# Moving the half swaps and the GELU steps of the S5 stream behind the attention steps in two engine queues

## Chip, cores and metric

The kernel runs on one core of a Trainium2 chip. The metric is the device time of one execution in microseconds (us); the figure of a kernel is the median of its runs.

## What is computed

A trunk of two residual layers over 2048 tokens of width 1024, with an RMSNorm at the end. The change touches only layer 0 (the even layer). It projects the normed input with one weight matrix and feeds two groups of heads:

```python
proj = h @ ev_w_in[i]
u, g_a, q, k, v, g_b = split_cols(proj, [...])
a_out = s5_mixer(u, ...) * jax.nn.silu(g_a)
b_out = swa_mixer(q, k, v, sinks, rel_bias) * jax.nn.silu(g_b)
mix = jnp.concatenate([a_out, b_out], axis=-1) @ ev_w_out[i]
```

`s5_mixer` is a diagonal complex state-space recurrence in 32 groups of 16 channels, followed by a GELU and a gated linear unit. `swa_mixer` is attention in 32 chunks of 64 queries, each over 128 keys, with a sink in the softmax. Layer 1 is a gated linear attention layer.

## The kernel before, in words

Each engine has its own in-order program, written out by hand, and the engines meet through semaphores. In the even layer every engine runs the same loop over a step counter `p` (0 to 147). Two steps make one accumulation `n = p // 2` of the input projection: in each step TensorE (PE) issues 12 products of 128x512 (line 1089), in three passes of high and low halves. There are 72 accumulations, so steps 0 to 143 have products. The last eight groups of weights (accumulations 40 to 71) are gates: ScalarE (ACT) takes a tanh (L638) and VectorE (DVE) finishes the gate (`silu`, L936). Other accumulations are copied out by ACT (L634). Three PSUM banks hold accumulations.

Into this loop two other pieces of work are woven, placed by small functions of `p`.

**The S5 stream**, one group `i` every three steps (`stream_at`), with `S_IN(0) = 40` and `S_OUT(0) = 43`:

- step 40+3i: PE `inputs(i)` (L1125), ACT `take_v(i)` (L675, L676, swaps the halves), DVE `scan(i)` (L942 to L945);
- step 41+3i: ACT `take_z(i)` (L682, L683, swaps the halves of the scan's result), DVE `turn_back(i)` (L954 to L956, writes `pz`);
- step 43+3i: PE `outputs(i)` (L1132, L1133), which waits for `pz` of group i and for `gelu_out(i-1)`, since both use one PSUM bank; ACT `gelu_square(i)` (L687);
- step 44+3i: DVE `gelu_arg(i)` (L960), ACT `gelu_tanh(i)` (L691);
- step 45+3i: DVE `gelu_out(i)` (L966). SyncE stores the result a step later.

`outputs(i-1)` and `inputs(i)` thus stand in the same step, one behind the other. The output steps are 43, 46, ..., 136. SyncE issues `load_stream(i)` (L375 to L379) at step 37+3i, once `outputs(i-2)` is done.

**The attention**, one chunk `c` every two steps (`chunk_at`), with `2*A0 = 80`:

- even step 80+2c: PE `scores(c)` (L1148), DVE `maxima(c)` (L984 to L990), ACT `exponents(c)` (L696, L698);
- odd step 81+2c: DVE `sums(c)` (L996, L997), ACT `copy_v(c)` (L718) and `normalize(c)` (L705), PE `turn_v(c)` (L1158);
- odd step 83+2c: PE `turn_p(c)` (L1165), ACT `copy_turned(c)` (L712);
- even step 84+2c: PE `values(c)` (L1175), DVE `take(c)` (L1004).

From step 80 to step 138 both are under way, and the pattern of the two repeats every six steps. Steps 16 to 49 also hold the making of the S5 tables (`powers_of_b`, `powers_of_c`, `copy_bm`, `copy_ker`). On PE each step runs its products first, then `outputs`, `inputs`, `values`, `scores`, `turn_p`, `turn_v`, as far as the step has them.

Of the kernel before, what the change touches and what calls it, by code (L numbers as in the profile page):

```python
# [151 lines left out]
def even_layer(nc, prm, scr, ht_hi, ht_lo, cst):  # L152
# [10 lines left out]
    S_IN, S_OUT = (lambda s: 40 + 3 * s), (lambda s: 43 + 3 * s)  # L163
# [4 lines left out]
    stream_at = lambda p, base: (p - base) // 3 if (p - base) % 3 == 0 and 0 <= (p - base) // 3 < NGRP else None  # L168
# [25 lines left out]
    with ExitStack() as ctx:  # L194
# [116 lines left out]
        with nc.Block() as block:  # L311
# [269 lines left out]
            def _(act):  # L581
# [34 lines left out]
                def evacuate(n):  # L616
                    g, b = accs[n]
                    act.wait_ge(acc_full, n + 1)
                    if g < G_K:
                        h = half_of(g, b)  # L620
                        if n < 8 and b >= 2:
                            act.wait_ge(u_stored[h], 16)
                        elif n >= 8:
                            act.wait_ge(u_stored[h], 32 if g == 2 else 48)
                        if n == 1:
                            act.wait_ge(zero_in, 16)
                        out = ustage[:, h].rearrange("p (s c) -> p c s", s=TS)[:, b % 2 * GLU_C:(b % 2 + 1) * GLU_C, :]
                        a.copy(out, acc[n % 3][:].rearrange("p (c s) -> p c s", s=TS)).then_inc(acc_free, 1)
                    elif n < N_GATE0:
                        if n < 20:  # L630
                            act.wait_ge(u_stored[n % 4 // 2], 64)
                        else:
                            act.wait_ge(stored[n % 4], 16 * (n // 4 - 4))
                        a.copy(stage[:, n % 4], acc[n % 3][:]).then_inc(acc_free, 1)  # L634
                    else:
                        if n > N_GATE0:
                            act.wait_ge(acc_free, n)
                        a.activation(th[:], acc[n % 3][:], ACT.Tanh, scale=0.5).then_inc(th_done, 1)  # L638
# [39 lines left out]
                def take_z(i):  # L678
                    act.wait_ge(z_ready, i + 1)
                    if i:  # L680
                        act.wait_ge(pz_ready, i)
                    a.mul(z_sw[0:ST], z[ST:P], -1.0).then_inc(z_swapped, 1)  # L682
                    a.copy(z_sw[ST:P], z[0:ST]).then_inc(z_swapped, 1)  # L683

                def gelu_square(i):
                    act.wait_ge(y_done, i + 1)
                    a.activation(e[:], ps_y, ACT.Square, scale=math.sqrt(0.044715)).then_inc(squared, 1)  # L687
# [20 lines left out]
                def copy_turned(n):  # L708
                    act.wait_ge(p_turned, n + 1)
                    if n:  # L710
                        act.wait_ge(o_done, n)
                    a.copy(pt[:], ps_p).then_inc(pt_ready, 1)  # L712
# [31 lines left out]
                evacuate(5)  # L744
                for p in range(13, p_end):
                    n = p // 2
                    i = stream_at(p, S_IN(0) + 1)
                    if i is not None:
                        take_z(i)
                    if p % 2 == 1 and n < n_acc:  # L750
                        evacuate(n)
                    c_ = chunk_at(p, 2 * A0 + 3)
                    if c_ is not None:
                        copy_turned(c_)
                    c_ = chunk_at(p, 2 * A0 + 1)
                    if c_ is not None:
                        copy_v(c_)
                        normalize(c_)
                    q = batch_at(p, TB + 1)
                    if q is not None:  # L760
                        copy_bm(q)
                    q = batch_at(p, TB + 2)
                    if q is not None:
                        copy_ker(q)
                    if p == 14:
                        split(2)
                    if p % 2 == 0 and n % 4 == 2 and n >= 10 and n // 4 + 1 < N_GRP:
                        split(n // 4 + 1)
                    i = stream_at(p, S_OUT(0) + 1)
                    if i is not None:  # L770
                        gelu_tanh(i)
                    i = stream_at(p, S_OUT(0))
                    if i is not None:
                        gelu_square(i)
                    i = stream_at(p, S_IN(0))
                    if i is not None:
                        take_v(i)
                    c_ = chunk_at(p, 2 * A0)
                    if c_ is not None:
                        exponents(c_)  # L780

            @block.vector
            def _(dve):
# [174 lines left out]
                def gelu_arg(i):  # L958
                    dve.wait_ge(squared, i + 1)
                    d.scalar_tensor_tensor(e[:], e[:], 1.0, ps_y, ALU.add, ALU.mult).then_inc(arg_ready, 1)  # L960

                def gelu_out(i):
                    dve.wait_ge(tanh_done, i + 1)
                    if i >= 2:
                        dve.wait_ge(g_st[i % 2], 16 * (i // 2))
                    d.scalar_tensor_tensor(go[:, i % 2], e[:], 1.0, ps_y, ALU.add, ALU.mult).then_inc(g_ready, 1)  # L966
# [10 lines left out]
                def maxima(n):  # L977
                    b = n % 2
                    dve.wait_ge(s_done, n + 1)
                    if n == 0:  # L980
                        dve.wait_ge(bias_in, 128)
                    if n >= 2:
                        dve.wait_ge(p_turned, n - 1)
                    ach.link(d.scalar_tensor_tensor(s[:, b], ps_s, DH ** -0.5, bias[:], ALU.mult, ALU.add))  # L984
                    if n == 0:
                        ach.link(d.memset(s[:, b, :, 0:CHUNK], -1e30))
                    ach.link(d.tensor_reduce(mx[:, b], s[:, b], AX_X, ALU.max))
                    ach.link(d.tensor_tensor(mx[:, b], mx[:, b], sink, ALU.max))
                    ach.mark(d.tensor_tensor(sd[:, b], sink, mx[:, b], ALU.subtract))
                    ach.link(d.tensor_scalar(mmx[:, b], mx[:, b], -1.0, None, ALU.mult))  # L990
                    dve.sem_inc(m_ready, 1)
# [30 lines left out]
                    pass  # L1022
                for p in range(12, p_end):
                    n = p // 2
                    i = stream_at(p, S_OUT(0) + 2)
                    if i is not None:
                        gelu_out(i)
                    i = stream_at(p, S_OUT(0) + 1)
                    if i is not None:
                        gelu_arg(i)  # L1030
                    if p % 2 == 0 and 0 <= silu_of(n - 1) and n - 1 < n_acc:
                        silu(n - 1)
                    c_ = chunk_at(p, 2 * A0 + 1)
                    if c_ is not None:
                        sums(c_)
                    c_ = chunk_at(p, 2 * A0 + 4)
                    if c_ is not None:
                        take(c_)
                    c_ = chunk_at(p, 2 * A0)
                    if c_ is not None:  # L1040
                        maxima(c_)
                    if p == 15:
                        split(2)
                    if p % 2 == 1 and n % 4 == 2 and n >= 10 and n // 4 + 1 < N_GRP:
                        split(n // 4 + 1)
                    q = batch_at(p, TB)
                    if q is not None:
                        powers_of_b(q)
                    q = batch_at(p, TB + 1)
                    if q is not None:  # L1050
                        powers_of_c(q)
                    q = batch_at(p, TB + 3)
                    if q is not None:
                        skip(q)
                    if p == S_IN(0) - 3:
                        for k in range(2):
                            dve.wait_ge(cs_st[k], CS_ALL // 2)
                        ch.link(d.memset(pz[:], 0.0))
                    i = stream_at(p, S_IN(0) + 1)
                    if i is not None:  # L1060
                        turn_back(i)
                    i = stream_at(p, S_IN(0))
                    if i is not None:
                        scan(i)
                    if p == TB + 2 * NQ + 6:
                        clear_keys()
                    if p == TB + 2 * NQ + 8:
                        distances()
# [1251 lines left out]
```

## Time and profile before

| | before |
|---|---|
| median of 3 runs | 1899.45 us (1895.48 to 1900.75) |
| the profiled execution, its own time | 1895.48 us |
| its span, first to last instruction | 1893.7 us |
| granted TensorE clock, mean | 0.965 of full |
| PE matmul busy | 1704.9 us, 90% |
| DVE busy | 842.9 us, 45% |
| ACT busy | 617.9 us, 33% |
| even layer's products (L1089) | 50.6 to 636 us |

Busy shares are averages over stages with different limits. The profile page slices the span, its timeline lists instructions in order with the idle time before each and what ended it in square brackets, and its table of waits sums those by pair. Engine names: PE is TensorE's matmuls, PEld its weight loads, SPq the SyncE queue that issues DMAs.

### The profile page before, as it was taken

Reading aid. Unit: us, or ns where it says so; the run is one execution under the profiler, and the core shown is the slowest. Engines: PE = TensorE matmul, PEld = TensorE weight load, DVE = VectorE, ACT = ScalarE, POOL = GpSimd, SP = SyncE. Lnnn points to the kernel's source line nnn. Section 1 sums busy time; section 2 is a strip of 40 time slices with the busy share of each in tenths; the row PEclk is TensorE's granted clock in tenths of the full one; section 3 lists DMA queues with packets and bytes.
Section 4 is the critical chain, followed back from the end, with each engine's and each line's share of the span. In section 5 each row is a group of like instructions: output and inputs, shape, how many; then the busy total and the mean of one; then the engine's idle time right before and its main releaser. Section 6 shows DMA issues by size and latency. Waiting matters only on the chain. (4 is left out here: it accounts for less than half of the span.)

```text
span 1893.7 us, 23556 instructions
## 1 busy us (share of the span) xinstructions
PE 1704.9 (90%) x7814; PEld 1365.8 (72%) x7814; DVE 842.9 (45%) x1677; ACT 617.9 (33%) x1587; POOL 398.3 (21%) x519
## 2 busy tenths in 40 slices
PE   1998897899999582998969999999999999979998
PEld 1776676777777371776856788888888888868886
DVE  3868443366666355233323323343333444343443
ACT  3622232366666431232324312222222233131211
POOL 0776000000000031875810002221222121000000
PEclk9999998999999796998979999999999999989999
DMA  7435444444544497555522333333333332265653
GB/s 173 143 110 158 119 126 125 134 133 133 151 140 129 129 314 245 180 154 165 178 67 84 106 109 109 109 114 104 116 111 118 97 112 84 84 209 161 191 179 110
DMA packets 316482, 261.03 MB, mean 138 GB/s; under 512 B 84344, under 2 KB 260280, under 8 KB 316376
## 3 DMA queue, kind: packets, MB, share of 16 engines
q1 hardware_dynamic: 299896, 249.13, 42.7%
q10 hardware_dynamic: 16480, 10.56, 1.9%
q8 instruction: 58, 0.95, 0.2%
q14 instruction: 48, 0.39, 0.1%
HBM read 157.33 MB, written 102.30 MB: 137 GB/s over the span
## 5 line engine op out<-in xcount | busy, mean ns | idle before, releaser
L2149 PE MATMUL odd_acc<-ht_hi,odd_w_hi 128*128 128x512 f32 x800 | 333.8, 417 | 8.5 <-DVE odd_w_hi L1986 8.5
L2149 PE MATMUL odd_acc<-ht_lo,odd_w_hi 128*128 128x512 f32 x800 | 315.3, 394 | 0.0
L2149 PE MATMUL odd_acc<-ht_hi,odd_w_lo 128*128 128x512 f32 x768 | 299.8, 390 | 0.0
L1089 PE MATMUL ev_acc<-ht_hi,ev_w_hi 128*128 128x512 f32 x576 | 244.5, 424 | 1.4 <-DVE ht_lo L801 1.4
L1089 PE MATMUL ev_acc<-ht_lo,ev_w_hi 128*128 128x512 f32 x576 | 228.4, 397 | 0.0
L1089 PE MATMUL ev_acc<-ht_hi,ev_w_lo 128*128 128x512 f32 x576 | 228.0, 396 | 0.0
L2149 PEld LDWEIGHTS odd_acc<-ht_hi,odd_w_hi 128*128 128x128 f32 x800 | 151.2, 189 | 49.6 <-DVE odd_w_hi L1986 8.7
L2149 PEld LDWEIGHTS odd_acc<-ht_lo,odd_w_hi 128*128 128x128 f32 x800 | 150.8, 188 | 33.8
L2001 DVE TENSOR_TENSOR odd_stage<-odd_acc,rms_rows 128x512 f32<-128x512 f32 x96 | 66.4, 692 | 229.3 <-PE odd_acc L2149 229.3
L2149 PEld LDWEIGHTS odd_acc<-ht_hi,odd_w_lo 128*128 128x128 f32 x768 | 144.6, 188 | 28.6
L1591 PE MATMUL out_acc<-wo_hi,mix_hi 128*128 128x512 f32 x256 | 107.0, 418 | 46.5 <-POOL mix_lo L1483 40.4
L1089 PEld LDWEIGHTS ev_acc<-ht_hi,ev_w_hi 128*128 128x128 f32 x576 | 110.5, 192 | 26.1 <-issue 3.3
L1303 POOL TENSOR_TENSOR glu_g_lo<-glu_g,glu_g_hi 128x2048 fp32r<-128x2048 f32 x4 | 22.2, 5539 | 508.7 <-ACT glu_g_hi L1315 508.7
L1089 PEld LDWEIGHTS ev_acc<-ht_lo,ev_w_hi 128*128 128x128 f32 x576 | 110.2, 191 | 24.9
L1089 PEld LDWEIGHTS ev_acc<-ht_hi,ev_w_lo 128*128 128x128 f32 x576 | 110.6, 192 | 21.3
L1915 ACT ACTIVATE odd_gl_o<-odd_gl_ps_o_s 128x256 f32<-128x256 f32 x64 | 24.6, 384 | 242.4 <-DVE odd_gl_state L2057 229.0
L1591 PE MATMUL out_acc<-wo_hi,mix_lo 128*128 128x512 f32 x256 | 102.7, 401 | 0.0
L1591 PE MATMUL out_acc<-wo_lo,mix_hi 128*128 128x512 f32 x256 | 102.7, 401 | 0.0
L1591 PEld LDWEIGHTS out_acc<-wo_hi,mix_hi 128*128 128x128 f32 x256 | 50.0, 195 | 60.1 <-POOL mix_lo L1483 41.7
L1857 POOL TENSOR_TENSOR odd_gl_var<-odd_gl_sumsq,odd_eps 128x1 f32<-128x1 f32 x64 | 21.8, 341 | 338.5 <-ACT odd_gl_o L1915 338.5
L1480 POOL TENSOR_TENSOR mix_hi<-mix_raw,xo_ones 128x1024 fp32r<-128x1024 f32 x32 | 76.5, 2391 | 62.7 <-PE out_acc L1591 46.4
L1507 ACT ACTIVATE ht_hi<-out_turned,xo_norm 128x128 f32 x128 | 36.5, 368 | 135.2 <-PE out_turned L1603 135.2
(297 smaller groups left out, 3172.9 us busy)
## 6 DMA issues: line engine op xcount, KB each, us to landing
odd_gl_in<-scr_heads SPq DMA_DIRECT2D x32, 640.0 KB, 4.3
mix_raw<-scr_mix SPq DMA_DIRECT2D x32, 512.0 KB, 4.1
scr_heads<-odd_stage SPq DMA_DIRECT2D x64, 256.0 KB, 2.0
odd_w_raw<-od_w_in SPq DMA_DIRECT2D x48, 256.0 KB, 3.5
ev_w_raw<-ev_w_in SPq DMA_DIRECT2D x36, 256.0 KB, 4.5
ev_x_tile<-x SPq DMA_DIRECT2D x16, 512.0 KB, 3.8
ev_s_cos_sin<-scr_s_cos_sin SPq DMA_DIRECT2D x32, 256.0 KB
xo_tile<-x SPq DMA_DIRECT2D x32, 256.0 KB, 4.5
```

Source lines behind the costliest of these rows:

```text
L1089: mm = pe.matmul(acc[n % 3][:], w[j][:, k, :], h[:, k, t], start=(k == 0 and r == 0), stop=(k == KT - 1 and r == 2))
L1303: nc.gpsimd.tensor_tensor(in_steps(g_lo[n % 2][:]), g[:, n], in_steps(g_hi[n % 2].ap().bitcast(F32)), ALU.subtract).then_inc(split, 1)
L1480: nc.gpsimd.tensor_tensor(m_hi[j][:], raw[:, j], ones[:].unsqueeze(1).broadcast_to([P, KT, P]), ALU.mult).then_inc(m_hi_done, 1)
L1507: m = nc.scalar.activation(ht_hi[:, KH * h + k, ds(t * P, P)], pt[j][:, k * P:(k + 1) * P], ACT.Copy, scale=norm_col[:, KH * h + k:KH * h ...
L1591: m = pe.matmul(acc[j][:], mt[j][:, k], wt[:, k], start=(k == 0 and q == 0), stop=(k == KT - 1 and q == 2))
L1857: g.tensor_tensor(var[:, j:j + 1], ss[:, j:j + 1], eps[:], ALU.add).then_inc(var_done, 1)
L1915: s.activation(on[:, j], ps_o[j], ACT.Square, scale=DV ** -0.5, accum_out=ss[:, j:j + 1]).then_inc(ss_done, 1)
L2001: v.tensor_tensor(stage[:, n % 4], acc[n % 4][:], rb[:, t], ALU.mult).then_inc(acc_free, 1)
L2149: mm = pe.matmul(acc[n % 4][:], w[j][:, k, :], h[:, k, t], start=(k == 0 and q == 0), stop=(k == KT - 1 and q == len(passes) - 1))
```

## The change

On ACT, `take_z` moves from the front of the step to a place behind the evacuation, the attention copies, the normalization, the table copies, the weight split, `gelu_tanh` and `gelu_square`; only `take_v` and `exponents` stand behind it. On DVE, `gelu_out` and `gelu_arg` move from the front of the step to a place behind `silu`, `sums`, `take` and `maxima`; `turn_back` and `scan` stay where they are, at the end. No instruction is added or removed, no wait is changed, and each of them stays in its step.

```diff
@@ ACT, for p in range(13, p_end)
-                    i = stream_at(p, S_IN(0) + 1)
-                    if i is not None:
-                        take_z(i)
                     if p % 2 == 1 and n < n_acc:
                         evacuate(n)
...
                     i = stream_at(p, S_OUT(0))
                     if i is not None:
                         gelu_square(i)
+                    i = stream_at(p, S_IN(0) + 1)
+                    if i is not None:
+                        take_z(i)
                     i = stream_at(p, S_IN(0))
                     if i is not None:
                         take_v(i)
@@ DVE, for p in range(12, p_end)
-                    i = stream_at(p, S_OUT(0) + 2)
-                    if i is not None:
-                        gelu_out(i)
-                    i = stream_at(p, S_OUT(0) + 1)
-                    if i is not None:
-                        gelu_arg(i)
                     if p % 2 == 0 and 0 <= silu_of(n - 1) and n - 1 < n_acc:
                         silu(n - 1)
...
                         maxima(c_)
+                    i = stream_at(p, S_OUT(0) + 2)
+                    if i is not None:
+                        gelu_out(i)
+                    i = stream_at(p, S_OUT(0) + 1)
+                    if i is not None:
+                        gelu_arg(i)
```

## Rows read from the trace of the kernel before

**Rows 1.** Busy time by stretch, with instructions in brackets, clock and DMA share.
```profile
core 0: us, PE busy (x) PEld busy (x) DVE busy (x) ACT busy (x) POOL busy (x), PEclk, DMA share, GB/s
400.00:500.00 100.00, 99.23 (x473) 76.00 (x472) 65.69 (x173) 66.72 (x233) 0.00 (x0) 1.00 0.48 143
```

**Rows 2.** PE's waits from 190 to 640 us: total us, times, longest.
```profile
PE ev_bank L1125 <- DMA ev_s_u<-scr_u: 17.7, 5, 9.6
PE ev_bank L1116 <- DVE ev_s_cpow L916: 4.7, 2, 4.0
```

**Rows 3.** Timeline of PE, 450 to 480 us: start, duration; products left out.
```profile
451.57 0.67 PE L1132 MATMUL ev_bank<-ev_s_u,ev_s_tables 128*128 128x256 f32 x2
...
453.62 1.13 PE L1148 MATMUL ev_bank<-ev_at_keys,ev_at_q 128*128 128x256 f32 x4
...
461.01 0.65 PE L1175 MATMUL ev_bank<-ev_at_probs_turned,ev_at_v_by_key 128*64 128x256 f32 x4 [0.18 <-issue]
...
465.32 0.59 PE L1132 MATMUL ev_bank<-ev_s_u,ev_s_tables 128*128 128x256 f32 x2
...
466.61 0.60 PE L1165 MATMUL ev_bank<-const_ident,ev_at_scores 128*128 128x128 f32 x4
...
477.66 0.67 PE L1132 MATMUL ev_bank<-ev_s_u,ev_s_tables 128*128 128x256 f32 x2
```

**Rows 4.** Timeline of ACT, 450 to 480 us.
```profile
467.77 0.57 ACT L712 COPY ev_at_probs_turned<-ev_bank 128x512 f32<-128x512 f32 x1
...
470.36 0.38 ACT L676 ACTIVATE ev_s_v_swapped<-ev_bank 64x256 f32<-64x256 f32 x1
472.75 0.42 ACT L682 ACTIVATE ev_s_z_swapped<-ev_s_z 64x256 f32<-64x256 f32 x1 [2.01 <-DVE ev_s_z L945]
...
473.62 0.42 ACT L691 ACTIVATE ev_s_gelu<-ev_s_gelu 128x256 f32<-128x256 f32 x1
475.84 0.20 ACT L696 ACTIVATE ev_at_small<-ev_at_small 128x4 f32<-128x4 f32 x1 [1.80 <-DVEq L991]
...
477.49 0.57 ACT L638 ACTIVATE ev_gate_tanh<-ev_acc 128x512 f32<-128x512 f32 x1
...
479.77 0.37 ACT L687 ACTIVATE ev_s_gelu<-ev_bank 128x256 f32<-128x256 f32 x1
```

**Rows 5.** Timeline of DVE, 450 to 480 us.
```profile
454.79 0.69 DVE L984 SCALAR_TENSOR_TENSOR ev_at_scores<-ev_bank,ev_at_bias 128x512 f32<-128x512 f32 x1 [0.63 <-PE ev_bank L1148]
...
456.82 0.42 DVE L942 TENSOR_TENSOR ev_s_v_turned<-ev_bank,ev_s_cos_sin 128x256 f32<-128x256 f32 x1
...
458.68 0.39 DVE L960 SCALAR_TENSOR_TENSOR ev_s_gelu<-ev_s_gelu,ev_bank 128x256 f32<-128x256 f32 x1
...
472.94 0.68 DVE L936 SCALAR_TENSOR_TENSOR ev_stage<-ev_gate_tanh,ev_acc 128x512 f32<-128x512 f32 x1
...
473.87 0.68 DVE L984 SCALAR_TENSOR_TENSOR ev_at_scores<-ev_bank,ev_at_bias 128x512 f32<-128x512 f32 x1
...
475.96 0.43 DVE L954 TENSOR_TENSOR ev_s_pz<-ev_s_z,ev_s_cos_sin 128x256 f32<-128x256 f32 x1 [0.21 <-DVE ev_at_small L990]
...
477.10 0.41 DVE L966 SCALAR_TENSOR_TENSOR ev_s_out<-ev_s_gelu,ev_bank 128x256 f32<-128x256 f32 x1
477.62 0.16 DVE L996 TENSOR_TENSOR ev_at_small<-ev_at_small 128x4 f32<-128x4 f32 x1
...
478.10 0.69 DVE L936 SCALAR_TENSOR_TENSOR ev_stage<-ev_gate_tanh,ev_acc 128x512 f32<-128x512 f32 x1
```

**Rows 6.** The SyncE queue's waits, 190 to 640 us.
```profile
SPq L375 <- PE ev_bank L1133: 33.5, 16, 4.3
```

**Rows 7.** Timeline of PE: two stalls, in brackets.
```profile
239.50 0.61 PE L1116 MATMUL ev_bank<-ev_s_cpow,ev_s_bbar 128*16 128x128 f32 x4 [3.98 <-DVE ev_s_cpow L916]
...
317.39 0.70 PE L1125 MATMUL ev_bank<-ev_s_u,ev_s_tables 128*128 128x256 f32 x2 [1.47 <-DMA ev_s_u<-scr_u]
```

**Rows 8.** Busy time by stretch, right behind those two stalls; PEclk is the granted clock.
```profile
239.50:242.00 2.50, 2.50 (x9) 1.89 (x10) 1.91 (x8) 0.84 (x3) 0.00 (x0) 0.68 0.62 194
...
317.30:320.00 2.70, 2.61 (x11) 2.18 (x12) 1.04 (x3) 0.74 (x2) 0.00 (x0) 1.00 0.63 215
```

## The prediction

> **What bounds the kernel now.** I read the busy time by stretch first. While S5 stream and attention run together PE is busy 99.2% of the time at full clock, against 66% for DVE and ACT [rows 1]. The even layer is bound by PE there, and a reordering of ACT and DVE can win only PE's idle time, or make some. PE's table of waits comes next: from 190 to 640 us it waits 17.7 us in 5 stalls for stream inputs from DMA and 4.7 us in 2 for the S5 tables [rows 2]. These lie ahead of the attention or at its edge. Inside it the timeline shows 0.18 us ahead of one `values` in each cycle of six steps [rows 3]. So at most some 2 us are to be won in the cycles, and the question is how much room PE's next operands have. The timelines of the three engines over one cycle answer it.
>
> The tightest operand is that of `outputs`, which needs `pz` and the preceding `gelu_out`. In the cycle shown `outputs` starts at 477.66 [rows 3]; its `gelu_out` starts at 477.10 and lasts 0.41 [rows 5], so it ends 0.15 us before. What the change puts ahead of `gelu_out` beyond 0.15 us becomes a stall of PE, once PE can't go around it.
>
> **The change part by part.** Nothing is added, so each engine's busy time stays. Ends move. Two kinds of `outputs` alternate, since three steps change the parity.
>
> *Intervals before.* From `outputs` in an odd step to the next, in an even step: 477.66 - 465.32 = 12.34 us, without a wait in it. From an even one to the next odd one: 465.32 - 451.57 = 13.75 us, with the 0.18 us in it [rows 3]. A cycle is 26.09 us.
>
> *Interval odd to even, after.* Count from the start of `outputs` (0). `turn_p` starts at 466.61 - 465.32 = 1.29 and ends at 1.89 [rows 3]. `copy_turned` starts at 1.93, and from there `copy_v`, `normalize`, `gelu_square` and `take_v` run on ACT in 470.74 - 467.77 = 2.97 us [rows 4]: 4.90. `scan` takes 458.68 - 456.82 = 1.86 from 4.93: 6.79. In the next (even) step DVE now begins with `silu` and `take`, 473.87 - 472.94 = 0.93: 7.72; from the start of `maxima` to whatever follows it are 475.96 - 473.87 = 2.09: 9.81 [rows 5]. PE's scores are ready before that (they end some 6.4 us after `outputs`), so they don't set it. Up to here little is new. What follows is: `gelu_arg` starts only now, 0.39 and 0.03 of handing on: 10.23. ACT has waited for it, although the maxima were ready, because `gelu_tanh` stands ahead of `exponents` in its queue. `gelu_tanh` 0.41: 10.64; `take_z` 473.62 - 472.75 = 0.87: 11.51 [rows 4]; then `exponents`, and `sums` 477.62 - 475.84 = 1.78 after their start [rows 4, 5]: 13.29; `sums` 0.48: 13.77; `gelu_out`, now behind `sums`, 0.41 and 0.04: 14.22. Before, `exponents` went straight behind `maxima`, and `gelu_out` did not wait for them at all. PE would be ready at 12.34: a stall of **1.88 us**.
>
> *Interval even to odd, after.* `scores` starts 453.62 - 451.57 = 2.05 after `outputs` and `maxima` 1.17 after that: 3.22 [rows 3, 5]. `exponents` follow `maxima`'s start by 475.84 - 473.87 = 1.97: 5.19, and hold ACT for 1.65: 6.84. In the odd step `evacuate`, `copy_turned`, `copy_v`, `normalize` take 479.77 - 477.49 = 2.28: 9.12 [rows 4]. `scan` and `sums` on DVE end before `normalize` starts (3.22 + 3.89 + 0.48 = 7.59), `gelu_arg` right behind. Then `gelu_tanh` 0.41 and `take_z` 0.87: 10.40. `take_z` used to go ahead of the four. What it delays is `turn_back`: 10.43 plus 477.10 - 475.96 = 1.14: 11.57 [rows 5]. `silu` and `take` 0.93: 12.50; `maxima` 2.09: 14.59; `gelu_out`, which used to go ahead of these three, 0.45: 15.04. Against 13.75 this is **1.29 us** more, the 0.18 us for `values` won back in it already, since `copy_turned` and `copy_v` no longer stand behind `take_z`.
>
> *How many.* Even output steps under attention: 82, 88, ..., 136, ten. Odd ones: 85, ..., 133, nine. The first one (82) has no `silu` or `take` ahead of it and I take 0.5 us less. Sum: 10 x 1.88 - 0.5 + 9 x 1.29 = 29.9 us. A stall also lets the others catch up, but that is in the count already: it runs around from `outputs` to `outputs`, and the cycle is then 29.3 us and no longer PE's. I left out the weight splits, 1 us on ACT and DVE every eighth step; in the new order they fall into time in which the engine waits. What is queued behind the late `gelu_out` and `take_z`: on DVE `split`, `turn_back`, `scan`; on ACT `take_v`, `exponents`. All are in the count. SyncE's store of the S5 result and the next `load_stream` move with `outputs`, and keep their three steps.
>
> *Steps 40 to 79.* Without attention `gelu_out` and `gelu_arg` have nothing new ahead of them. `take_z` goes behind an evacuation (0.48) and `gelu_tanh` (0.41) in an odd step, but has two more steps of PE's products before `outputs`, over 5 us: nothing. With the tables (41, 44, 47) it goes behind `copy_bm` or `copy_ker` too, while PE's table waits total 4.7 us [rows 2]. Bounds: 1 us won (evacuations and copies earlier), 3 lost (1 us each, if a `turn_back` pushes out a table step). I take 0, nearest to what the stalls show: they end with DVE steps that stay ahead of `turn_back`.
>
> *Clock.* After a stall of 1.47 us the granted clock is 1.00, that is 2.4 GHz; after one of 3.98 us it is 0.68 over 2.5 us, part of it at 1.2 GHz [rows 7, 8]. The stalls expected are at the first kind, so the sum has nothing for it. The Trainium skill ("TensorE: Matmul & The Clock Gate", section "A second HAM failure mode: psum-queue depth-cycling") tells of a kernel whose TensorE idled only briefly but often between groups of matmuls and whose clock still swung between its two levels. By the row the clock costs nothing here, by that rule it costs the second rival's price below.
>
> **Rivals.** (1) *Only one side stalls.* The even-to-odd chain has 22 steps and exceeds PE by 1.3 us; with 0.05 us less at each hand-over it is 1 us shorter and nearly hidden, and 18 to 20 us remain: 1914. For it: my ACT durations are ends, and the next instruction starts some 0.1 us earlier; against: the chain reproduces what the trace shows before `maxima`. (2) *The clock falls.* After the 3.98 us stall 9 matmuls were issued in 2.5 us where full clock has some 12.5 [rows 8], so twice 3.5 matmuls in 5 us, at 0.23 us 1.6 us a stall: with 19 stalls 30 us more, 1956. Against it: the stall of 1.47 us. (3) *The other side: faster.* `evacuate` no longer waits behind `take_z`, SyncE's stores and with them its queue move up, stream loads arrive earlier, and part of the 17.7 us goes away [rows 2]; all of it would give 1878. It decides if those loads are issued late because of a store ahead of them. Against it: SyncE's wait at the head of the load is for `outputs` on PE, 33.5 us in 16 [rows 6]. And it would have to outweigh the stalls. (4) *Nothing happens:* other limits I misread leave `gelu_out` in time, as in steps 40 to 79; then only 2 us are won, 1894 in the profiled execution. Against it: the 0.15 us.
>
> **How the numbers follow.** The profiled execution took 1895.48 us; with 30 it gives 1925.4. The median of the three runs is 4.0 us above it, which gives 1929.4. I say 1928. The forecast (both sides stall, clock full) has 0.78, rival 1 0.08, rival 2 0.07, rival 3 0.03, rival 4 0.04. Chain lengths uncertain by 0.6 us each make 19 x 0.6 = 11 us, the table steps -1 to +3, runs 4: 1912 to 1946, which takes in rival 1 and leaves out the others. Differences within 0.3% (5.7 us) can't be told from none. Slower by more: 0.92; within: 0.05; faster: 0.03.
>
> **What would show it.** In the changed kernel's PE waits, L1132 should wait for DVE's `gelu_out` 19 times, about 1.9 and 1.5 us in turn, some 30 us in all; the 0.18 us ahead of `values` should be gone; even outputs should follow each other by 29.3 us; the exponents should start 1.7 us later after the maxima in every third attention step; `gelu_out` should start right behind `sums` or `maxima`. Steps before 80 should take as long as before, with the same DMA stalls, and everything after the even layer should only shift. PEclk should stay at 10 tenths between 370 and 660 us. The prediction is wrong if `outputs` waits for `pz` rather than `gelu_out`, if the clock falls behind these stalls, or if the stalls by DMA grow or vanish.

## The result

The changed kernel takes 1929.12 us (median of 4 runs, 1926.30 to 1931.81) against 1900.10 us for the one before (4 runs): a ratio of 1.0157 (95% interval 1.0136 to 1.0180), 30 us slower. The profiled execution took 1925.92 us with a span of 1924.1 us, 30.4 us more than before. The forecast of 1928 us and its direction held.

The profile after, first by stretch. The busy times of PE, DVE and ACT in the attention stage are what they were; only the stage is longer:

```profile
370.00:670.00 300.00, 267.79 (x1264) 202.81 (x1262) 173.02 (x460) 177.95 (x630) 0.00 (x0) 1.00 0.40 117
```

The granted clock, third from the end, is 1.00 over all of it. The same stretch of the kernel before, up to 640 us, holds 266.23 us of PE work. Where the 30.4 us arise is told by the start of `outputs` in its last step ahead of the attention (step 79: 353.91 us after, 355.11 before) and in its very last step (136: 638.56 after, 608.25 before). Between the two lie 284.65 us after and 253.14 before: the stage is 31.5 us longer, 1.2 us were gained ahead of it, and 0.1 us arises behind it.

PE's waits from 190 to 690 us, as [rows 2] (total, times, longest):

```profile
PE ev_bank L1132 <- DVE ev_s_out L966: 30.5, 19, 1.7
PE ev_bank L1125 <- DMA ev_s_u<-scr_u: 17.9, 5, 8.9
PE ev_bank L1116 <- DVE ev_s_cpow L916: 4.5, 2, 3.6
```

The first row is new: `outputs` (L1132) waits for `gelu_out` (L966), 19 times, 30.5 us. The other two are as in [rows 2]. Three `outputs` in a row in the timeline of PE, as in [rows 3]:

```profile
462.30 0.67 PE L1132 MATMUL ev_bank<-ev_s_u,ev_s_tables 128*128 128x256 f32 x2 [1.69 <-DVE ev_s_out L966]
...
477.46 0.67 PE L1132 MATMUL ev_bank<-ev_s_u,ev_s_tables 128*128 128x256 f32 x2 [1.53 <-DVE ev_s_out L966]
...
491.67 0.67 PE L1132 MATMUL ev_bank<-ev_s_u,ev_s_tables 128*128 128x256 f32 x2 [1.70 <-DVE ev_s_out L966]
```

Even to odd 15.16 us (13.75 before), odd to even 14.21 us (12.34 before), a cycle of 29.37 us (26.09 before). The way from an odd to an even `outputs`, on ACT and then on DVE, as in [rows 4, 5]:

```profile
482.08 0.38 ACT L676 ACTIVATE ev_s_v_swapped<-ev_bank 64x256 f32<-64x256 f32 x1
487.73 0.42 ACT L691 ACTIVATE ev_s_gelu<-ev_s_gelu 128x256 f32<-128x256 f32 x1 [5.28 <-DVE ev_s_gelu L960]
488.18 0.42 ACT L682 ACTIVATE ev_s_z_swapped<-ev_s_z 64x256 f32<-64x256 f32 x1
488.62 0.40 ACT L683 COPY ev_s_z_swapped<-ev_s_z 64x256 f32<-64x256 f32 x1
489.05 0.20 ACT L696 ACTIVATE ev_at_small<-ev_at_small 128x4 f32<-128x4 f32 x1
```

```profile
485.26 0.68 DVE L984 SCALAR_TENSOR_TENSOR ev_at_scores<-ev_bank,ev_at_bias 128x512 f32<-128x512 f32 x1
...
487.28 0.42 DVE L960 SCALAR_TENSOR_TENSOR ev_s_gelu<-ev_s_gelu,ev_bank 128x256 f32<-128x256 f32 x1
...
490.83 0.16 DVE L996 TENSOR_TENSOR ev_at_small<-ev_at_small 128x4 f32<-128x4 f32 x1 [0.55 <-ACT ev_at_scores L698]
491.03 0.18 DVE L997 RECIPROCAL ev_at_small<-ev_at_small 128x4 f32<-128x4 f32 x1
491.12 0.40 DVE L966 SCALAR_TENSOR_TENSOR ev_s_out<-ev_s_gelu,ev_bank 128x256 f32<-128x256 f32 x1
```

ACT is idle for 5.28 us, with `take_z` and then the exponents queued behind; it waits for `gelu_arg` (L960), which DVE runs behind the maxima (L984). Only then come `gelu_tanh` (L691), `take_z` (L682, L683) and the exponents (L696), 3.79 us after the maxima's start instead of 1.97 [rows 4, 5]. `sums` (L996) wait for the exponents, `gelu_out` stands behind them, ends at 491.52, and PE starts at 491.67.

The way from an even to an odd `outputs`, from 462.30 to 477.46:

```profile
467.49 0.21 ACT L696 ACTIVATE ev_at_small<-ev_at_small 128x4 f32<-128x4 f32 x1 [1.77 <-DVEq L991]
...
471.43 0.41 ACT L691 ACTIVATE ev_s_gelu<-ev_s_gelu 128x256 f32<-128x256 f32 x1
```

```profile
472.74 0.43 DVE L954 TENSOR_TENSOR ev_s_pz<-ev_s_z,ev_s_cos_sin 128x256 f32<-128x256 f32 x1 [1.54 <-ACT ev_s_z_swapped L683]
...
476.89 0.42 DVE L966 SCALAR_TENSOR_TENSOR ev_s_out<-ev_s_gelu,ev_bank 128x256 f32<-128x256 f32 x1 [0.21 <-DVE ev_at_small L990]
```

The exponents are in time here. `gelu_tanh` and then `take_z` stand behind the copies and the normalization, so `turn_back` (L954) is late, and behind it `silu`, `take`, the maxima and `gelu_out`.

PE starts 0.15 us after the end of `gelu_out` here (491.52 to 491.67), and 0.14 or 0.15 us at every one of the 19 waits. That is what handing on from DVE to PE takes. In the kernel before it is 0.15 us at the `outputs` of [rows 3] as well (477.51 to 477.66), and at eight of the ten even `outputs`. So PE had no slack there: it already waited for `gelu_out`, by a little. The timeline doesn't show that in brackets, for this reason (the last two products ahead of `outputs`, before, then after):

```profile
477.14 0.39 PE L1089 MATMUL ev_acc<-ht_hi,ev_w_lo 128*128 128x512 f32 x1
477.36 0.39 PE L1089 MATMUL ev_acc<-ht_lo,ev_w_hi 128*128 128x512 f32 x1
```

```profile
489.35 0.39 PE L1089 MATMUL ev_acc<-ht_hi,ev_w_lo 128*128 128x512 f32 x1
489.58 0.39 PE L1089 MATMUL ev_acc<-ht_lo,ev_w_hi 128*128 128x512 f32 x1
```

A product's record lasts 0.39 us, but the next one starts 0.23 us behind it. The brackets count from the end of the record, so they leave out the first 0.16 us of a wait. `outputs` came 0.30 us behind the last product before, a hidden wait of 0.07 us, and 2.09 us behind it after, a wait of 1.86 us of which the brackets show 1.70.

### The profile page after: what moved, and what is told of

It is laid out like the page before. It is cut to its first block and busy times, and to the rows that moved or that the text cites. A ratio compares the mean times of both kernels' runs of the same rounds, so it can differ in the third digit from the quotient of the medians.

```text
span 1924.1 us, 23556 instructions
## 1 busy us (share of the span) xinstructions
PE 1706.3 (89%) x7814; PEld 1364.2 (71%) x7814; DVE 842.7 (44%) x1677; ACT 619.7 (32%) x1587; POOL 398.3 (21%) x519
## 5 line engine op out<-in xcount | busy, mean ns | idle before, releaser
L1591 PE MATMUL out_acc<-wo_hi,mix_hi 128*128 128x512 f32 x256 | 107.2, 419 | 47.2 <-POOL mix_lo L1483 41.2
L1591 PE MATMUL out_acc<-wo_hi,mix_lo 128*128 128x512 f32 x256 | 102.8, 401 | 0.0
L1591 PE MATMUL out_acc<-wo_lo,mix_hi 128*128 128x512 f32 x256 | 102.8, 401 | 0.0
L1591 PEld LDWEIGHTS out_acc<-wo_hi,mix_hi 128*128 128x128 f32 x256 | 50.1, 196 | 60.8 <-POOL mix_lo L1483 42.5
```

Of the source, the lines that this page charges most:

```text
L1591: m = pe.matmul(acc[j][:], mt[j][:, k], wt[:, k], start=(k == 0 and q == 0), stop=(k == KT - 1 and q == 2))
```

## The experiments

Each ratio is against runs of the kernel before made alongside, at 1895.5 to 1896.4 us (1900.1 for the change). "Forecast" is what was expected for the whole kernel, in us against the kernel before, with its range; "by ratio" is the same as measured. "Stage" is how much longer the way from the `outputs` of step 79 to the last one (step 136) is than before, in the one trace of each kernel. "Cycle" is the distance of every second `outputs` in the timeline between 440 and 500 us; nine such cycles lie between steps 82 and 136. No experiment leaves out any work.

| kernel | ratio to before (95%) | forecast | by ratio | stage | even to odd | odd to even | cycle, us |
|---|---|---|---|---|---|---|---|
| before | 1 | | | | 13.75 | 12.34 | 26.09 |
| the change | 1.0157 (1.0136 to 1.0180) | 30 | 30 | 31.5 | 15.16 | 14.21 | 29.37 |
| ACT's part only | 1.0053 (1.0036 to 1.0069) | 7 (3 to 9) | 10 | 7.0 | 13.46 | 13.37 | 26.83 |
| DVE's part only | 1.0063 (1.0046 to 1.0080) | 9.5 (6 to 12) | 12 | 9.3 | 13.85 | 13.21 | 27.06 |
| `gelu_out` only | 1.0040 (1.0026 to 1.0055) | 4 (0 to 6) | 8 | 5.3 | 13.86 | 12.73 | 26.59 |
| `gelu_arg` only | 1.0016 (1.0001 to 1.0031) | 0 (-2 to 2) | 3 | 1.7 | 13.97 | 12.28 | 26.25 |
| change, `gelu_out` back | 1.0142 (1.0125 to 1.0159) | 20 (16 to 23) | 27 | 25.5 | 13.47 or 15.06 | 14.74 | 28.2 or 29.8 |
| change, outputs last on PE | 1.0158 (1.0141 to 1.0175) | 0 (-3 to 3) | 30 | 26.1 | 12.6 or 13.8 | 15.5 or 16.0 | 28.1 to 29.8 |
| DVE's part, tanh last on ACT | 1.0017 (1.0007 to 1.0026) | 0.5 (-1 to 3) | 3 | 3.3 | 13.86 | 12.43 | 26.29 |
| change, tanh last on ACT | 1.0072 (1.0048 to 1.0096) | 9 (6 to 12) | 14 | 11.6 | 14.85 | 12.43 | 27.28 |
| change, tanh and outputs last | 1.0038 (1.0022 to 1.0054) | -1 (-3 to 2) | 7 | 4.1 | 12.26 | 13.99 | 26.25 |
| before, `take_z` ahead of `normalize` | 0.9991 (0.9978 to 1.0005) | -1.6 (-3 to 1) | -2 | -2.1 | 13.46 | 12.37 | 25.83 |

By their times seven of the ten variants came out above their ranges, one lies at the upper end and two inside. A trace also differs by some us where the kernels are the same: the first `inputs` (step 40, ahead of every edit) starts between 202.3 and 205.4 us, and from the last one to the end it takes 0.5 us less to 3.2 us more than before where the clock does not fall. One trace each can't tell that from chance. The chain of the forecasts runs inside the stage only, and there the four kernels that move single pieces give 7.0, 9.3, 5.3 and 1.7 us, within every range.

### The two parts alone

**ACT's part only.** The first hunk of the change, without the second.

```diff
-                    i = stream_at(p, S_IN(0) + 1)      # ahead of evacuate
-                        take_z(i)
...
                         gelu_square(i)
+                    i = stream_at(p, S_IN(0) + 1)
+                        take_z(i)
```

> Only ACT's part of the change: take_z behind the evacuation, copies, normalization and GELU steps; DVE as before. The theory of the prediction (one chain from outputs to outputs, counted step by step): turn_back comes later, but gelu_out stays ahead of silu, take and maxima, so odd outputs find it done; the later turn_back pushes DVE's silu, take and maxima of the next even step from 1.65 us ahead of the odd outputs to 0.7 us ahead, ACT carries that on, and the even outputs come 13.2 us after the odd ones where PE needs 12.34: ten stalls of 0.8 us at L1132, none at odd outputs, the 0.18 us ahead of values gone. In all +7 us (3 to 9). Rival A (each move has a price of its own and the two parts add up to the 30 us): the ACT part and the DVE part together give 30, so one of them gives at least 15. Rival B (only the lateness of gelu_out behind attention work counts, and ACT's part is free): 0 here and 30 for DVE's part.

Measured: 1.0053, some 10 us, just above the range of 3 to 9; the interval of the ratio reaches down to 7 us, and the stage is 7.0 us longer. The cycle grows by 0.74 us, of which 13.37 - 12.34 = 1.03 us is in the odd-to-even interval (0.8 forecast). PE's waits from 370 us on show where:

```profile
PE ev_bank L1132 <- DVE ev_s_out L966: 4.4, 9, 0.5
...
PE ev_bank L1158 <- DVE ev_at_out L1004: 2.0, 8, 0.3
```

Only every second `outputs` waits, but the second row was not in the chain: `turn_v` (L1158) waits for `take`, which the later `turn_back` delays.

**DVE's part only.**

```diff
-                        gelu_out(i)                    # front of the step
-                        gelu_arg(i)
...
                         maxima(c_)
+                        gelu_out(i)
+                        gelu_arg(i)
```

> Only DVE's part of the change: gelu_out and gelu_arg behind silu, sums, take and maxima; ACT as before. Theory of the chain: take_z stays at the front, so the 0.87 us of take_z go out of the chain behind gelu_arg, and the even outputs come 13.35 us after the odd ones: ten stalls of 1.0 us; before the odd outputs gelu_out is done at 13.53 us where PE comes at 13.75: no stall. In all +9.5 us (6 to 12). Rival A (parts add up): with the ACT-only kernel 30 us in all. Rival B (all of it is DVE's part): +30 us, stalls of 1.7 and 1.5 us at all nineteen.

Measured: 1.0063, some 12 us (forecast 9.5, range to 12), and 9.3 us in the stage. Odd to even 13.21 us where the chain gave 13.35, even to odd 13.85 for 13.75. The waits in the table are again at every second `outputs`:

```profile
PE ev_bank L1132 <- DVE ev_s_out L966: 6.4, 10, 0.7
```

The odd `outputs` start 0.15 us behind `gelu_out` here too. They are just late enough for a hidden wait; the 0.1 us is what the forecast "no stall" had missed.

The two parts give 10 + 12 = 22 us, the whole 30; in the stage they give 7.0 + 9.3 = 16.3 us, the whole 31.5. Rival A (the parts add up) falls 8 us short, or 15 by the stage, rival B (all of it DVE's) by far more. Together the parts do what neither does alone: they make the odd `outputs` wait as well, since there `take_z` puts `turn_back` late and `turn_back` puts the maxima late, ahead of which `gelu_out` no longer stands.

**`gelu_out` only, `gelu_arg` only.**

```diff
-                        gelu_out(i)                    # the one kernel; gelu_arg(i) stays
...
                         maxima(c_)
+                        gelu_out(i)
```

```diff
-                        gelu_arg(i)                    # the other; gelu_out(i) stays
...
                         maxima(c_)
+                        gelu_arg(i)
```

> Only gelu_out moved behind silu, sums, take and maxima; gelu_arg and take_z as before. Theory of the chain: gelu_tanh comes early, the exponents go straight behind the maxima, only sums (0.48 us, and its wait for the exponents) stand ahead of gelu_out in the odd step: even outputs 12.7 us after odd ones, stalls of 0.4 us, +4 us in all (0 to 6), none at the odd outputs. Rival B (the place of gelu_out alone makes the loss): near +30 us.

> Only gelu_arg moved behind silu, sums, take and maxima; gelu_out and take_z as before. Theory of the chain: gelu_tanh and the exponents start 0.45 us later after the maxima, but gelu_out at the front of the next step is done 11.8 us after the odd outputs, before PE's 12.34: no stall, 0 us (-2 to +2). Rival A (each move costs its own share): some +10 us.

`gelu_out` alone: 1.0040, 8 us by the time (above the range of 0 to 6), 5.3 us in the stage, odd to even 12.73 where 12.7 was forecast. `gelu_arg` alone: 1.0016, 3 us (above -2 to 2), 1.7 us in the stage, no wait in the table at any `outputs`; what it costs is 0.2 us ahead of `values` at twice as many places as before, which I had left out:

```profile
PE ev_bank L1175 <- issue: 2.7, 16, 0.2
```

The two make 11 us apart and 12 us together, 7.0 and 9.3 us in the stage. The chain predicted the order and the places of the waits. By the times it was low by 2.5 to 4 us in each of the four kernels, by the stage off by 0.2 us or less in two, 1.3 us and 1.7 us low in these.

### What in it costs

**The change with `gelu_out` back in front.**

```diff
+                        gelu_out(i)                    # front of the step, as before
...
                         maxima(c_)
-                        gelu_out(i)
```

> The changed kernel with gelu_out alone put back to the front of DVE's step; gelu_arg and take_z stay moved. Theory of the chain: odd outputs find gelu_out done (no stall), but the maxima of the even step ahead of them start 0.7 us before the odd outputs and ACT is late from there on; take_z and the exponents behind gelu_tanh make the even outputs come 14.6 us after the odd ones: ten stalls of 2.2 us, longer than in the changed kernel. In all +20 us over the kernel before (16 to 23). Rival B (gelu_out behind the attention steps is the cause): all of the 30 us come back, 0.

Measured: 1.0142, 27 us, above the range of 16 to 23. Rival B (all of the 30 us come back) is refuted: putting back the very instruction for which PE waits returns 3 us of 30, and the intervals of the two ratios overlap. The waits are as forecast, ten, nine of them 2.1 to 2.2 us long:

```profile
PE ev_bank L1132 <- DVE ev_s_out L966: 20.0, 10, 2.2
```

No odd `outputs` waits any more, so `gelu_out` behind the maxima does make the odd waits of the change; the even ones grew from 1.7 to 2.2 us. The waits at `outputs` thus fell from 30.5 to 20.0 us. Part of that gain is lost again elsewhere. From an even `outputs` to the next odd one it takes 13.47 us in some cycles and 15.06 in others (459.05 to 474.11 in the timeline), with no wait in either. The busy time by stretch, right behind three of the stalls:

```profile
430.80:433.30 2.50, 2.46 (x12) 1.64 (x13) 2.34 (x5) 2.50 (x9) 0.00 (x0) 1.00 0.00 0
...
459.00:461.50 2.50, 2.45 (x10) 1.35 (x10) 1.03 (x3) 2.50 (x9) 0.00 (x0) 0.74 0.50 163
461.50:464.00 2.50, 2.50 (x8) 1.82 (x7) 0.57 (x2) 1.83 (x4) 0.00 (x0) 0.58 0.58 161
...
633.00:635.50 2.50, 2.35 (x9) 1.18 (x10) 1.12 (x4) 2.50 (x9) 0.00 (x0) 0.75 0.70 219
635.50:638.00 2.50, 2.50 (x7) 2.00 (x8) 0.92 (x2) 0.10 (x1) 0.00 (x0) 0.56 0.32 100
```

Behind the second one the granted clock fell, to 0.58 over 2.5 us, that is to the lower level (1.2 GHz) for most of it, and PE issued 8 matmuls where the first row has 12. It fell behind four of the nine long stalls, at the `outputs` of steps 100, 112, 124 and 136. Three of them lie inside the stage and cost 1.6 us each, 4.8 us; with the 20.0 us of waits that is nearly all of the 25.5 us in the stage. The fourth, at 633 us, is at the last `outputs`, and from there on this trace is 4.1 us longer than the one before; if the fourth fall costs 1.6 us too, 2.5 us are left open. The prediction's second rival had exactly this price, though the change itself does not pay it.

**DVE's part, with the tanh behind the exponents.**

```diff
 # ACT
-                        gelu_tanh(i)                   # ahead of gelu_square
...
                         exponents(c_)
+                    i = stream_at(p, S_OUT(0) + 1)
+                        gelu_tanh(i)
```

> DVE as in the changed kernel (gelu_out and gelu_arg behind the maxima), ACT as before but gelu_tanh behind the exponents. Theory of the chain: what costs in DVE's part is that gelu_tanh waits for the late gelu_arg at the head of ACT's queue with the exponents behind it. With the exponents ahead, gelu_out is done 12.4 us after the odd outputs, PE needs 12.34: stalls of 0.1 us or none, +0.5 us (-1 to +3). Rival B (gelu_out behind maxima and sums costs by its place): as much as DVE's part alone.

Measured: 1.0017, 3 us (the upper end of the range), where DVE's part alone costs 12. The even `outputs` come 12.43 us after the odd ones, forecast 12.4. `gelu_out` is as far behind maxima and sums as in DVE's part; only the exponents no longer wait behind a `gelu_tanh` that waits. So of the 12 us some 9 come from the head of ACT's queue.

**The whole change, with the tanh behind the exponents.** The same edit on top of the change.

> The whole change, with one thing different: on ACT gelu_tanh goes behind the exponents (take_z stays where the change put it). Theory: most of the loss hangs on the exponents, which stand behind gelu_tanh, which waits for the late gelu_arg. With the exponents ahead, the even outputs come 12.4 us after the odd ones (stall 0.1 us); the odd outputs are reached by the other chain (take_z late, turn_back, silu, take, maxima, gelu_out) and stall 1.0 us, nine times. In all +9 us over the kernel before (6 to 12), so some 21 of the 30 us come back. Rival B (gelu_out behind the attention steps costs by its place): the 30 us stay.

Measured: 1.0072, 14 us by the ratio, above the range of 6 to 12; 11.6 us in the stage and 11.3 us by the table of waits, forecast 9:

```profile
PE ev_bank L1132 <- DVE ev_s_out L966: 11.3, 9, 1.3
```

The even `outputs` are free but for a hidden wait of about 0.1 us, the odd ones still wait, 1.2 to 1.3 us each (1.5 in the change, 1.0 forecast). The place of `gelu_tanh` ahead of the exponents on ACT is worth 16 of the 30 us. What stays is the other chain, the waits at the odd `outputs`. It needs both moves: with `gelu_out` back these waits are gone, and with DVE's part alone, `take_z` in time, they are 0.1 us.

**The whole change, with `outputs` and `inputs` last in PE's step.**

```diff
 # PE
-                        outputs(i)
-                        inputs(i)                      # ahead of values, scores, turn_p, turn_v
...
                         turn_v(c_)
+                        outputs(i)
+                        inputs(i)
```

> The changed kernel, and on PE the outputs and inputs of a step behind values, scores, turn_p and turn_v instead of ahead of them. No work differs. Theory of the chain: the loss is that PE, stopped at outputs, holds back the attention operands that the chain itself waits for. With outputs last, scores and transposes are not held back, both chains are then some 12.3 us (odd to even, PE needs 12.34) and 12.4 us (even to odd, PE needs 13.6): no stall or below 0.2 us each, 0 us against the kernel before (-3 to +3). Rival C (gelu_out and take_z are simply late by a fixed amount, whatever PE does): outputs come only 0.7 to 1.6 us later in the step, stalls shrink by that and 5 to 15 us stay.

Measured: 1.0158, 30 us. My theory expected 0 and rival C 5 to 15; both were wrong. PE's waits show what I had left out:

```profile
PE ev_bank L1175 <- ACT ev_at_probs_turned L712: 20.3, 11, 2.0
...
PE ev_bank L1132 <- DVE ev_s_out L966: 1.6, 9, 0.3
```

The wait at `outputs` is all but gone, as computed, and stands now at `values` (L1175), which needs `copy_turned` (L712). `copy_turned` follows the exponents on ACT, with only the gate's tanh between, and these are as late as in the change. In the timeline of that kernel `values` starts late, and behind four of nine such stalls the clock falls too, ahead of the same steps 100, 112, 124 and 136:

```profile
460.88 0.65 PE L1175 MATMUL ev_bank<-ev_at_probs_turned,ev_at_v_by_key 128*64 128x256 f32 x4 [1.99 <-ACT ev_at_probs_turned L712]
461.46 1.66 PE L1148 MATMUL ev_bank<-ev_at_keys,ev_at_q 128*128 128x256 f32 x4
462.91 1.06 PE L1132 MATMUL ev_bank<-ev_s_u,ev_s_tables 128*128 128x256 f32 x2
```

The granted clock is 0.72 from 460.8 us on and 0.59 in the next 2.5 us. (`scores` take 1.13 and the pair at L1132 0.67 us at full clock.) The theory had to be sharpened: it is not `gelu_out` that is late but ACT, and `outputs` was only the first of PE's operands to show it.

**Both: tanh behind the exponents, outputs last.** This tells the sharpened theory from "outputs last costs by itself".

> The whole change, gelu_tanh behind the exponents, and on PE outputs and inputs behind the attention pieces of the step. Outputs-last alone left the loss at 30 us and moved PE's wait to values, which waits for copy_turned behind the late exponents. Theory: with the exponents in time both are served. values has 1.1 us to spare, the odd outputs come 13.6 us after the even ones with gelu_out done at 12.0: no stalls at L1132 or L1175 inside the cycles, -1 us (-3 to +2) against the kernel before. Rival C (outputs last costs by itself, for instance by a later y): +5 us or more stays.

Measured: 1.0038, 7 us, above the range of -3 to 2 and inside rival C's "+5 us or more". Most of the 30 us is gone, and the cycle is 26.25 us with no wait at `outputs`. Its two halves are not as I had them: the odd `outputs` come 12.26 us after the even ones and not 13.6. `values` still waits once a cycle, 0.46 us at 459.14, where I had counted 1.1 us to spare. The stage is 4.1 us longer than before, 1.7 us of it between the `outputs` of steps 79 and 82 and the rest in the cycles. The trace is 10.6 us longer in all, more than the 7 us of the ratio. Most of the difference lies ahead of the attention: the `outputs` of step 79 starts at 361.11 us in this execution against 355.11 before. Of these 6 us 2.5 are there at the first `inputs` already (205.39 against 202.90, step 40), ahead of which the two kernels do not differ, so they are not the edit's. 1.9 are a longer wait at step 55, 2.7 us instead of 0.8 for the attention's small inputs, since `outputs` and `inputs` stood ahead of that wait before:

```profile
PE ev_bank L1137 <- DMA ev_at_small<-swa_sinks: 2.7, 1, 2.7
```

The remaining 1.6 us are not traced to a cause. The kernel with outputs last alone has the same 2.7 us wait and reaches step 79 at 356.98 us, 1.9 us behind. So rival C is right to that much: outputs last costs by itself, some 2 us ahead of the attention; how much more of the 7 us is its own stays open.

**Before, with `take_z` behind `copy_v` and ahead of `normalize`.** The experiments point at one small gain: the 0.18 us ahead of `values` [rows 3].

```diff
-                        take_z(i)                      # ahead of evacuate
...
                         copy_v(c_)
+                        take_z(i)
                         normalize(c_)
```

> The kernel before, and only take_z moved, not behind everything but behind copy_v and ahead of normalize. Theory: copy_turned and copy_v come ahead of it, so the 0.18 us ahead of values go away at nine places; turn_back is 0.9 us later at odd steps, which DVE has, since gelu_out waits for gelu_tanh there anyway. -1.6 us (-3 to +1), a cycle of 25.9 us in the trace; too small for the time. Rival: any delay of turn_back is carried on as with ACT's whole part, +3 to +7 us.

Measured: 0.9991 with an interval over 1 (0.9978 to 1.0005). In the trace the cycle is 25.83 us, 0.26 us shorter, and `values` has no wait inside it. The stage is 2.1 us shorter, too little for the times to tell. It is the fastest of the kernels here, by its trace.

## Why the prediction was right

- *What bounds the stage.* Right: PE, at full clock. All time lost lies in PE's waits there: the table has 30.5 us of them.
- *The slack of 0.15 us.* Misread. The 0.15 us between the end of `gelu_out` and PE's start is the handing on, and the same where PE waits. The even `outputs` had no slack before and a hidden wait of 0.07 us, so "PE would be ready at 12.34" is `gelu_out`'s time and not PE's own. It did no harm to the sum, which compares intervals that were both read or built with `gelu_out` in them.
- *Odd to even, 14.22 us forecast.* 14.21 measured. The single steps agree to 0.1 us too: the exponents start 3.79 us after the maxima (11.51 - 7.72 = 3.79 in the sum). That the end agrees to 0.01 us is luck: the sum has 0.04 us for handing on to PE, where it takes 0.15, and has `gelu_out` end 0.12 us late (14.18 for 14.06), since `sums` hold it up for 0.29 us and not 0.48.
- *Even to odd, 15.04 us forecast.* 15.16 measured. The exponents (5.19), `gelu_tanh` (9.13 for 9.12), `turn_back` (10.44 for 10.43) and `gelu_out` (14.59) start as counted to 0.01 us; the missing 0.12 us is the handing on to PE.
- *The number.* 19 waits, in turn 1.7 and 1.5 us. The sum had 1.88 and 1.29, the signs "about 1.9 and 1.5"; the intervals grew by 1.87 and 1.41, and the brackets leave out 0.16 us of each wait. The first one, at step 82, shows 1.22 us. The stage grew by 31.5 us where the sum gave 29.9, and 1.2 us came back ahead of it. The signs also had the exponents 1.7 us later after the maxima, where the sum's own figures give 3.79 - 1.97 = 1.82, which is what came.
- *The clock.* Right for this kernel: 1.00 over the whole stage. The rival was nearer than I gave it. Stalls of up to 1.7 us left the clock alone 19 times, those of 2.2 us brought it down in four of nine cases in one kernel, those of 2.0 us in four of nine in the other. What the Trainium skill tells of in the section cited there ("TensorE: Matmul & The Clock Gate", "A second HAM failure mode: psum-queue depth-cycling"), a clock that swings while TensorE idles briefly and often, did not show in the changed kernel and did in these two.
- *Steps 40 to 79.* Right: the same waits in number, their sums within 0.3 us, and `outputs` of step 79 at 353.91 us against 355.11 before. But PE's waits for the S5 tables come to 9.5 us in four and not to 4.7 in two, since [rows 2] leave out two rows of that view. One of them is a wait for ACT's `copy_ker` (L669), so not all of these stalls end with DVE steps. After the change they come to 9.5 us too (4.5 + 3.9 + 1.1). The rows before:

```profile
PE ev_bank L1116 <- ACT ev_s_kernel L669: 3.6, 1, 3.6
PE ev_bank L1108 <- DVE ev_s_bpow L901: 1.2, 1, 1.2
```

- *The rivals.* One side only, faster, and nothing are refuted by the 19 waits in turn; the loads by DMA, which rival 3 would have moved, still cost 17.9 us. The row against rival 3 was weaker than it looked: in SyncE's queue before, the longest waits are those of a store for `silu`, which the change moves up, and not those of the load [rows 6]:

```profile
SPq L339 <- DVE ev_stage L936: 86.2, 20, 8.2
```

  They come to 84.0 us after, so little moved.
- *What was not right.* The prediction told the story of `outputs` and the bank it shares. The runs show that this is where the loss is seen, and that two chains make it. At the even `outputs` it is ACT's queue: `gelu_tanh` waits at its head for 5.28 us, then comes `take_z`, with the exponents behind them; `gelu_tanh` behind the exponents gives back 16 of the 30 us and all even waits of the table. At the odd ones it is `take_z` behind four attention steps together with `gelu_out` behind the maxima; take either back and these waits are gone, or are 0.1 us. Both chains stood in the sum. What the prediction did not have is that `values` stands right behind: with `outputs` relieved, it waits for the same late exponents. For the four kernels that move single pieces the sums were 2.5 to 4 us low against the times, by the stage 1.7 us at most. The rest lies outside the stage. In the traces of ACT's part and of `gelu_arg` alone it is mostly a wait far behind it, of PE for GpSimd (L1591 for L1483: 42.7 and 43.1 us for 40.4), where the kernels do not differ; whether that is chance stays open.

## What to carry to other kernels

In a loop written out by hand for in-order engines, an instruction moved "later, it has time" brings the instructions behind it along: look for one that will wait at the head of a queue, and count what stands behind it on the way to the bound engine. Count the whole way round, from one operand of that engine to the same operand next time, and do it for every operand with little slack: if one is relieved, the next takes over (here `values` for `outputs`, with the same 30 us). Costs of such moves need not add: two moves of 10 and 12 us made 30, and undoing the one at which PE waits gave back 3. Before counting a gap between two engines as slack, look how long the gap is where the second engine does wait; here it was the same 0.15 us.

## What was not expected of the hardware

The granted clock did not fall behind any of 19 stalls of 1.2 to 1.7 us, each 14 to 15 us after the last. With stalls of 2.1 to 2.2 us every 28 to 30 us it fell behind four of nine, and with stalls of 2.0 us behind four of nine, at a price of 1.6 us where it can be read. In both kernels it fell at the same steps, 100, 112, 124 and 136, every second stall, some 58 us apart, and not at 88 and 94. The stalls differ in length and in spacing, and no run here varies one alone, so which of the two matters is not shown.

PE starts `outputs` 0.14 to 0.15 us after the reported end of the DVE instruction it waits for, in each of the 19 waits of the changed kernel, and 0.14 to 0.16 us in the variants with such waits. ACT and DVE start 0.03 to 0.04 us after each other's end (`gelu_tanh` at 487.73 after `gelu_arg`, which ends at 487.70; `turn_back` at 489.06 after `take_z`, which ends at 489.02).
